# Attention rows turned ahead of the first dense portion of a step

## The reference, cut to what matters

```python
def mem_attend(cq, mk, mv, q_norm):
    q = head_rms(cq.reshape(B, L, MEM_HEADS, MEM_HEAD_DIM), q_norm)
    s = jnp.einsum('blhd,bmhd->bhlm', q, mk) * MEM_HEAD_DIM ** -0.5
    p = jax.nn.softmax(s, axis=-1)
    return jnp.einsum('bhlm,bmhd->blhd', p, mv).reshape(B, L, MEM_WIDTH)

def swa_prompt(q, k, v, sinks):          # window of 128, 12 query heads on 4 key heads
    s = jnp.einsum('bnqkgd,bnskd->bnkgqs', qb, kk) * SW_HEAD_DIM ** -0.5
    p = sink_softmax(jnp.where(mask, s, NEG), sinks)
    return jnp.einsum('bnkgqs,bnskd->bnqkgd', p, vv)

x = x + jnp.concatenate([tok, mo], axis=-1) @ w_out[i]
x = x + (jax.nn.silu(g) * u) @ w_ffn_out[i]
```

## Time and profile before

| What | Value |
|---|---|
| median of three runs | 3090.18 us |
| the profiled execution, its own time | 3087.6 us |
| span of its trace | 3085.8 us |
| PE busy | 2909.1 us, 94% |
| DVE, ACT, POOL busy | 1300.4, 692.9, 640.7 us |
| mean granted clock of PE | 0.952 of full |
| pair 0, 94 to 190 us: PE busy, granted clock | 89.47 of 96 us, 0.90 |
| pair 1, 1695 to 1805 us | 101.03 of 110 us, 0.86 |
| pairs 2 to 4, 1885 to 2237 us | 325.06 of 352 us, 0.89 |

### The profile page before, as it was taken

How to read it: one execution, slowest core, us unless ns; L and a number is a source line. 1 busy time by engine, 2 the same in 40 slices (tenths; PEclk the granted TensorE clock), 3 DMA queues, 4 the chain that set the end, 5 groups by cost and what they waited for, 6 DMA issues and landing times.

```text
span 3085.8 us, 42287 instructions
## 1 busy us (share of the span) xinstructions
PE 2909.1 (94%) x16482; PEld 2597.9 (84%) x16482; DVE 1300.4 (42%) x2195; ACT 692.9 (22%) x1164; POOL 640.7 (21%) x322
## 2 busy tenths in 40 slices
PE   5999999998899999999988979999889999999998
PEld 5779888897799999999977678877779999999997
DVE  4233444434544444444454323353454444444444
ACT  4421121211411111111123412343441111111110
POOL 5003332222421111221114000000042111112210
PEclk8989999999899999999998889898899999999999
DMA  4111011111121111121102010101011211111211
GB/s 154 29 55 49 23 41 49 49 36 29 42 55 41 41 41 41 41 54 47 54 21 69 28 55 21 21 21 45 15 35 49 54 41 41 41 41 41 56 32 57
DMA packets 186027, 135.37 MB, mean 44 GB/s; under 512 B 19616, under 2 KB 175456, under 8 KB 185888
## 3 DMA queue, kind: packets, MB, share of 16 engines
q1 hardware_dynamic: 181760, 129.69, 15.2%
q10 hardware_dynamic: 4160, 4.19, 0.4%
HBM read 124.61 MB, written 11.27 MB: 44 GB/s over the span
## 4 chain that ended last, share of the span: by engine, by line
PE 83%; PEld 6%; DVE 5%; issue 2%; ACT 2%; POOL 2%; PEldq 1%; DMA 0%; SPq 0%; DVEq 0%; ACTq 0%
PE ps L1364 44%; PE ps L1401 24%; PEld ps L1364 3%; PE ps L1526 2%; PE ps L1551 2%; PEld ps L1671 2%; PE ps L1390 1%; POOL w_lo L509 1%; PE ps L1536 1%; PE ps L1616 1%; PE ps L1582 1%; DVE x L938 1%; DVE normed_gained L935 1%; ACT w_hi L505 1%; PE ps L1514 1%
## 5 line engine op out<-in xcount | busy, mean ns | idle before, releaser
L935 DVE TENSOR_TENSOR x<-x,ps 128x512 f32<-128x512 f32 (+1 forms) x882 | 604.2, 686 | 882.4 <-PE ps L1401 877.3
L509 POOL TENSOR_TENSOR w_lo<-w_raw,w_hi 128x1024 fp32r<-128x1024 f32 x194 | 464.9, 2417 | 2182.9 <-ACT w_hi L505 2182.9
L1364 PE MATMUL ps<-hT_hi,w_hi 128*128 128x352 f32 x2976 | 723.8, 332 | 12.1 <-POOL w_lo L509 10.3
L1364 PE MATMUL ps<-hT_lo,w_hi 128*128 128x352 f32 x2976 | 713.9, 328 | 0.0
L1364 PE MATMUL ps<-hT_hi,w_lo 128*128 128x352 f32 x2976 | 710.3, 328 | 0.0
L1364 PEld LDWEIGHTS ps<-hT_hi,w_hi 128*128 128x128 f32 x2976 | 524.6, 192 | 49.7 <-POOL w_lo L509 10.8
L1364 PEld LDWEIGHTS ps<-hT_lo,w_hi 128*128 128x128 f32 x2976 | 526.4, 192 | 29.7 <-issue 2.0
L1364 PEld LDWEIGHTS ps<-hT_hi,w_lo 128*128 128x128 f32 x2976 | 525.7, 191 | 26.5 <-issue 1.3
L1401 PE MATMUL ps<-w_hi,m_hi 128*128 128x512 f32 (+1 forms) x1072 | 437.0, 408 | 20.8 <-POOL w_lo L509 9.0
L1401 PE MATMUL ps<-w_lo,m_hi 128*128 128x512 f32 (+1 forms) x1072 | 430.5, 402 | 0.0
L1401 PE MATMUL ps<-w_hi,m_lo 128*128 128x512 f32 (+1 forms) x1072 | 428.2, 399 | 0.0
(11 more groups left out here) (220 smaller groups left out, 2486.2 us busy)
## 6 DMA issues: line engine op xcount, KB each, us to landing
w_raw<-in_w_ffn_in_dram SPq DMA_DIRECT2D x176, 256.0 KB, 3.2
w_raw<-in_w_ffn_out_dram SPq DMA_DIRECT2D x88, 256.0 KB, 3.7
w_raw<-in_w_in_hgrn_dram SPq DMA_DIRECT2D x52, 256.0 KB, 4.6
w_raw<-in_w_out_dram SPq DMA_DIRECT2D x32, 256.0 KB, 3.9
w_raw<-in_w_in_swa_dram SPq DMA_DIRECT2D x24, 256.0 KB, 4.2
x<-in_x_prompt_dram SPq DMA_DIRECT2D x8, 512.0 KB, 9.4
w_raw<-in_w_mem_kv_dram SPq DMA_DIRECT2D x16, 256.0 KB, 5.6
cache<-in_cache_mem_k_dram SPq DMA_DIRECT2D x4, 1024.0 KB, 7.2
```

The source lines that it names most:

```text
L509: nc.gpsimd.tensor_tensor(slot(1, s), raw[:, j3, :], slot(0, s).bitcast(F32), ALU.subtract).then_inc(w_lo, 1)
L935: return V_.tensor_tensor(out, a, b, op)
L1364: return mmul(ps[:, b0 + g, 0:TW], slot(a, s)[:, P * k:P * k + P], hT[b][:, k, TW * g:TW * g + TW], start=m < 3, stop=m >= 69)
```

## The change

`prompt_out`, the turn, moves within a step of `pair`: from behind the samples' pieces, just ahead of `fill(s, 1)`, to just behind the prompt's scores, ahead of `fill(s, 0)`. The lists of ACT, DVE, POOL and SP stay as they are, and PE has as many instructions as before.

```diff
@@ -1636,6 +1636,8 @@
                         prompt_turn(r - 2)
                     if s < ROUNDS:
                         prompt_scores(r, window)
+                    if s >= 4 and s % 2 == 0:
+                        prompt_out(r - 3)
                     fill(s, 0)
                     if S_SSC <= s < S_SSC + NB:
                         sample_scores(p, s - S_SSC, window)
@@ -1645,8 +1647,6 @@
                         sample_turn(p, window)
                     if s == S_SPV:
                         sample_rows_mm(p, window)
-                    if s >= 4 and s % 2 == 0:
-                        prompt_out(r - 3)
                     fill(s, 1)
```

## The result

| | before | after |
|---|---|---|
| median of six runs | 3090.39 us | 3106.66 us |
| range | 3086.89 to 3093.22 | 3100.30 to 3110.16 |
| profiled execution | 3087.6 us, span 3085.8 | 3100.3 us, span 3098.5 |
| PE busy, rest of the span | 2909.1 and 176.7 us | 2919.4 and 179.1 us |
| mean granted clock of PE | 0.952 | 0.948 |

The change makes the kernel slower: the ratio is 1.0050, 95% interval 1.0037 to 1.0063, 16.3 us between the medians. The forecast was 3096.7 us in a range up to 3105: right in sign, wrong in size.

What follows compares the result with a forecast made beforehand. PE's in-order list was taken to bound the kernel, with the key copy as late link. Terms 1.1 + 2.1 + 0.6 + 2.1 + 1.2 - 0.6 = +6.5 us gave 3096.7 us, 0.21% slower; range 3089.5 to 3105.

Steps and rivals of the forecast that it cites:

- The order's terms: Shifts of PE against the chain m_hi, m_lo, rows, priced step by step: +6.5 us in sum.
- the rows of step 5 to those of step 7 in pair 1: Steps 4 and 6 of pairs 0 and 1, step 10 of pair 1: key copy 0.22 us later each, 1.1 us.
- the extra change of tile shape: Five steps without a portion: 0.22 us plus 0.20 for a gap of the samples' scores, 2.1 us in all.
- Windows: Steps 4, 6 and 8 of pairs 2 to 4: no reserve, 0.07 us for each of 9 turns, 0.6 us.
- Step 12 of pair 1: Work that ran in the turn's wait for attn_rows now stands behind it: 2.1 us, up to 4.2 at half clock.
- Step 18: Pairs 2 and 3: the turn loses the portion that hid the division and waits 0.59 us each, 1.2 us.
- Gains: Steps 12 and 14 of pair 0, step 14 of pair 1: turn is the late link, 0.2 us each, -0.6 us.
- The mechanism behind the sign: Slower, chance 0.50: the early turn delays the cached keys' transposes, hence the key copy ahead of m_hi in ACT's list.
- the clock falls further: Rival, 22%: longer waits at step 12 of pair 1 or step 10 bring another half-clock stretch; +11.5 us, 3101.7 us.
- the argument against: Against that clock rival: the stretch behind step 12 of pair 1 is already low and may merely begin earlier.
- The test that the prediction set itself: Five pairs: low clock stretches changing by more than 10 us in all would mean the clock, not the order, decided.
- The lower ends: All terms at their smallest: +3.5 us, 3093.7 us; in a run as fast as the fastest before, 3089.5 us.

Runs made afterwards that it cites:

- e7: Kernel before with the cached keys' transposes right behind the prompt's scores, turn early at steps to 10 and three later places: -16.3 us, ratio 0.9946.
- e14: Kernel before with the turn early at steps 4 and 6 of pair 1 only: +6.4 us, ratio 1.0014.
- e1: Kernel before with the turn early in pair 1 only: +7.0 us, ratio 1.0023.
- e16: Kernel before with the turn early in pair 1 and 14 identity transposes in the wait of its step 8: +2.1 us, ratio 1.0006.
- e3: Kernel before with the turn early in pairs 2 to 4 only: +5.7 us, ratio 1.0018.
- e2: Kernel before with the turn early at step 12 of pair 1 only: +5.7 us, ratio 1.0020.
- e8: Kernel before with the turn early only at steps 12 and 14 of pair 0 and step 14 of pair 1: +7.6 us, ratio 1.0024.
- e13: Kernel before with the turn early at step 8 of pair 1 only: +8.2 us, ratio 1.0024.
- e4: Kernel before with the turn early in pair 0 only: +3.0 us, ratio 1.0011.
- e10: Kernel before, order unchanged, with 8 extra identity transposes in pair 0, step 1: +1.9 us, ratio 1.0001.
- e11: Kernel before, order unchanged, with 32 extra identity transposes in pair 0, step 1: +3.2 us, ratio 1.0011.
- e6: Changed kernel with forty identity transposes in the turn's wait at step 12 of pair 1: +12.2 us against the kernel before, ratio 1.0038.

## Why the prediction was wrong in size

*The order's terms held, one by one.* At full clock, from rows to rows: the rows of step 5 to those of step 7 in pair 1 went from 11.97 to 12.17 us, +0.20 (0.22 in the sum). The rows of step 7 to those of step 9, with the extra change of tile shape, from 11.64 to 12.01, +0.37 (0.42). Windows: 25.95 to 26.00 over two turns, +0.03 each (0.07). Step 12 of pair 1: the turn's wait grew by 2.06 (2.1). Step 18: a wait of 0.52 each (0.59). Gains: 6.29 to 5.98 and 9.41 to 9.11 in pair 0, 0.3 each (0.2). Pairs 0 and 2, whose half clock stayed as it was within half a us, grew by 0.4 and 0.7 us, about their terms. That changing the tiling mode drains TensorE, as the Trainium skill has it in "TensorEngine Tiling (Array Packing)", section Key Properties, agrees with the 0.17 us gap behind so short a pair of matmuls. The mechanism behind the sign, the key copy in ACT's list ahead of m_hi, is shown by the trace and by e7: with the keys first the wait of rows 3 is gone.

*The step that failed is the clock.* The sum let each term cost its own length, and kept the granted clock for the upper end of one term (4.2 us at step 12) and for one rival, "the clock falls further": one more stretch, at step 12 or step 10, 5 us, 22%. It was the larger part: in the traces 10.3 us of the 12.7 are longer busy time of PE, and over the runs the lower clock took 14.6 us more. The two parts don't simply add, which the sum had also left out: PE's idle time grew by 2.4 us and not by 6.5, since waits vanish where the matmuls ahead of them run at half clock (pair 4, step 10 to 18). The rival's place was wrong as well. Step 12, with the longest new wait, lost nothing within pair 1 up to step 14: the half clock began earlier there and was shorter, which the prediction had named as the argument against. The stretch came behind step 8, after waits that had grown by 0.2 us each. The mistake was to look for the half clock behind long waits only, because rows 9 stood behind one, and to take its stretches as given elsewhere. Several short waits close together matter too (e14), and 13.12 us at 0.87 in before showed that this place was already losing 3.4 us to half clock between two waits of 1.44 us.

In the Trainium skill, "TensorE: Matmul & The Clock Gate", section "A second HAM failure mode: psum-queue depth-cycling", tells of a kernel whose short idle times between groups of matmuls make the clock swing. e1 and e16 agree: 18.1 and 11.7 us for the same work, without and with a filled wait.

*The test that the prediction set itself* said that the clock, not the order, has set the result if the low stretches in the five pairs change by more than 10 us. They changed by 23, from 92 to 115 us: by its own test the sum by the order was the wrong sum.

*A slip in the range.* The lower ends less the 3.3 us of the fastest run before give 3090.4 us, not 3089.5. It changes nothing here, the result lies above the upper end.

*What stays open.* Why the change as a whole costs 10 us more than its order. Only pair 1 is explained, and that in the main: 5 of its 7.2 us are the stretch behind step 8; 1.8 more lie between its last two rows, at half clock as well (13.27 to 15.04 us, clock 0.79 to 0.69), and what called these is not shown. Pair 3 has 2.8 us more in the changed kernel and in e3, which have the same windows, but also 2.2 to 2.5 more in e2, e8, e13 and e14, whose windows are those of before. e8, e13 and e14 have 41.3 to 41.4 us in pair 4 where before, e1, e2, e4, e10 and e11 have 35.68. Whether such distant stretches belong to a kernel or to a single execution, one trace of each can't tell; nor is it known what in the execution decides.

## What to carry to other kernels

Before moving a piece forward, find what its consumer waits for: here a copy that stood ahead in ACT's list. Moving that one's source gave 13 us, where moving the turn alone lost 16. When a change alters the time, split the span into busy and idle time of PE first; more busy time for the same matmuls is the clock. In a kernel that is 94% busy, don't price a few tenths of a microsecond of new idle time at their own length where the granted clock of that stretch is already below 1: one early turn with 0.2 us of longer wait made 13.1 us into 17.9 here. And before reading an effect out of one trace, compare stretches that the change can't have touched: here they differed by 3 us and more.

## What the runs showed of the hardware

- The same 170 matmuls of pair 4, in the order of before, took 35.68 us in six traces (before, e1, e2, e4, e10, e11; mean granted clock 0.79 or 0.80) and 41.28 to 41.42 in three (e8, e13, e14; 0.62). In the order of the changed kernel they took 36.80, 38.96, 38.98 and 45.50 (0.72, 0.66, 0.66, 0.52). What decides between them is not shown.
- Where the half clock falls isn't fixed by the instructions ahead: up to the end of pair 0, e2, e14 and e16 are the kernel before, and took 3.0 us longer in that pair.
- Useless work can pay, at least locally: 14 transposes in a wait shortened 18.1 us to 11.7 (e1, e16). A transpose of 128x128 takes 0.11 us in a row of 32 or 40 (e11, e6).
- A turn right behind the prompt's scores has a gap of 0.33 us of its own; the gap doesn't add up but moves, since at step 12 of pair 0 it takes the place of the one that the portion had the earlier trace rows. Ahead of the samples' scores there is another 0.17 us.
